# Two unread 512-column matmuls ahead of the scores of every attention unit

## The chip, the cores and the metric

The kernel runs on one core of a Trainium2 chip, as one program written by hand in Bass: each engine has its own list of instructions, and semaphores order them against each other. The metric is the device time of one execution in microseconds, of which the median of several is given. Lower is better.

## What is computed

Two transformer blocks on 256 tokens of width 1024. The first mixes three things (differential attention, an RWKV-7 time mix, attention over a memory of 256 rows) and ends in a mixture of 16 experts; the second has two layers, each with feed-forward, a mixer and feed-forward. All values are float32. What matters here are the four kinds of attention, which share one pipeline in the kernel:

```python
# first block: differential attention, 4 heads, two maps each, causal
s = einsum('bhmqd,bhmkd->bhmqk', qb, kh)          # head size 64
p = softmax(where(causal, s + bias, MASK_VALUE))
attn = p[:, :, 0] - lam * p[:, :, 1]
out = einsum('bhqk,bhke->bhqe', attn, vh)
# first block: attention over the memory, 4 heads
p = softmax(einsum('bshd,bmhd->bhsm', q, mk) * 64 ** -0.5)
# second block, even layer: dilated mixture (8 heads) and top-k attention (8 heads)
# second block, odd layer: sliding window with a learned sink per head, 16 heads
```

Around them stand products of the 256 tokens with large weight matrices: the projections into and out of each mixer, the experts and the feed-forwards.

## The kernel before

**Weights.** Every weight matrix is cut into slots of 128 rows by 3072 columns. SyncE loads them in turn into `raw`; ScalarE rounds a slot to fp32r (`w_hi`, L507) and VectorE stores the rest of the rounding (`w_lo`, L825). TensorE multiplies high by high, low by high and high by low (`mm3`, L1341 to L1343), so each product of float32 is three fp32r matmuls. The tokens lie transposed in `xT_hi` and `xT_lo`, fp32r too: 8 blocks of 128 partitions by 256 tokens each, rewritten by `norm` ahead of each group of projections.

**Attention.** The attention work is cut into 44 units. A unit is 128 query rows (tile `t`, 0 or 1) of one pair of heads, or of the two maps of one differential head; with `nk` key blocks of 128, which is `t + 1` in causal units, so that units alternate between one block (even numbers) and two (odd). The memory units always have two. Four calls of `attention(u0, u1)` run them: units 0 to 11 (8 differential, 4 memory; called the first attention below), 12 to 19 and 20 to 27 (the even layer: dilated, then top-k; the second and third), and 28 to 43 (the odd layer; the fourth). A unit goes through these steps, each on one engine:

- TensorE, `scores_unit`: two matmuls, one for each head (or map), L1403. Their operands are 64 partitions high and plain float32, and each shows in the trace as two records of 128 or 256 columns. They write PSUM banks `2 * (u % 2)` and the one after it.
- VectorE, `max_unit`: adds the bias into SBUF (L861, L864 or L870), takes the row maximum (L872), and for the fourth attention adds the sink (L875).
- ScalarE, `exp_unit`: exponential and row sum (L557), for the fourth attention that of the sink too (L560). In differential units VectorE then combines the two maps (L882 to L885).
- TensorE, `trans_unit`: transposes of 128 by 128 through the identity matrix (`flip`, L1347), into bank `4 + u % 2`.
- ScalarE, `evac_unit`: copies them to SBUF (L569).
- TensorE, `pv_unit`: probabilities by values, L1431, two records to a matmul.
- VectorE, `out_unit`: divides by the row sum and stores the result (L897 to L899, or L893).

**The order of the work** is written out by hand. TensorE's `attention` goes, for each `i`, through the scores of unit `i`, the transposes of unit `i - 2` and the product with the values of unit `i - 3`. ScalarE goes through the exponential of `i` and the evacuation of `i - 2`; VectorE through the maximum of `i`, in the second attention also two rounds of the search for the top 64 keys, and the output of `i - 4`. Each engine runs its list strictly in this order. The scores of unit `u` wait (`att_max`) until VectorE has read those of unit `u - 2`, since the two share their banks.

After an attention, `norm` transposes its result, 16 transposes at L1347, and the output projection follows.

Of the kernel before, what the change touches and what calls it, by code (L numbers as in the profile page):

```python
# [23 lines left out]
P = 128  # L24
# [72 lines left out]
def block_program(nc, wstream, x_in, mem_in, pos_in, pos_cols_in, pcol_in, prow_in, smallw_in, const_in, table_in, bias_lookup_in,  # L97
                  bias_dram, out):
    ctx = ExitStack()
    with ctx:  # L100
        def sb(name, shape, dt=F32):
            return ctx.enter_context(nc.sbuf_tensor(name, shape, dt))
# [3 lines left out]
        def S_(name):  # L106
            if name not in sems:
                sems[name] = ctx.enter_context(nc.semaphore(name))
            return sems[name]
# [5 lines left out]
        xT_hi = sb("xT_hi", [P, KD, S], F32R)  # L115
# [13 lines left out]
        ps = ctx.enter_context(nc.psum_tensor("ps", [P, 8, 512], F32))  # L129
# [1206 lines left out]
        def _(pe):  # L1336
            mm = nc.tensor.matmul
# [8 lines left out]
            def flip(out_, in_):  # L1346
                return nc.tensor.transpose(out_, in_, ident)  # L1347

            def norm(c, wait=None):
                n = norms[c]  # L1350
                if n["norm"]:
                    pe.wait_ge(S_("xs_ready"), normed[c] + 1)
                    pe.wait_ge(S_("xs1_ready"), normed[c] + 1)
                if wait:
                    pe.wait_ge(S_(wait[0]), wait[1])
                src = scaled if n["norm"] else n["src"]
                for q in range(4):
                    for k in (2 * q, 2 * q + 1):
                        for t in range(T):
                            o = S * (k % 2) + P * t  # L1360
                            ins = flip(ps[:, 4 + q, o:o + P], src[:, t, P * k:P * k + P])
                    ins.then_inc(S_("tr_ready"), 1)
# [33 lines left out]
            def scores_unit(u):  # L1396
                un = units[u]
                w, t = un["nk"] * P, un["t"]
                if u >= 2:
                    pe.wait_ge(S_("att_max"), u - 1)  # L1400
                for m in range(2):
                    o = slice(HD * m, HD * m + HD)
                    ins = mm(ps[:, 2 * (u % 2) + m, 0:w], un["q"][o, P * t:P * t + P], un["k"][o, 0:w], start=True,  # L1403
                             stop=True)
                ins.then_inc(S_("att_scores"), 1)
# [28 lines left out]
            def attention(u0, u1):  # L1434
                for i in range(u0, u1 + 3):
                    if i < u1:
                        scores_unit(i)
                    if u0 <= i - 2 < u1:
                        trans_unit(i - 2)
                    if u0 <= i - 3 < u1:  # L1440
                        pv_unit(i - 3)
# [127 lines left out]

            pe.wait_ge(S_("ident_loaded"), 16)  # L1570
            norm(0)

            pe.wait_ge(S_("const_loaded"), 16)
# [53 lines left out]
            for i in range(len(LEVELS) - 1):  # L1627

                pe.wait_ge(S_("lev_ready"), i + 1)
                for g in range(T):  # L1630
                    pe.wait_ge(S_("inv_ready"), 2 * i + g + 1)
                    for u in range(4):
                        ins = mm(ps[:, g, P * u:P * u + P], levt[i % 2][:, 4 * g + u, :], inv[:, 4 * g + u, :],  # L1633
                                 start=True, stop=True)
# [47 lines left out]
            for n in range(QKV0, MEM0):  # L1682
                proj(n)
            norm(1, ("evacuated", evac_until(MEM0 - 1)))
            for n in range(MEM0, OUT0):
                proj(n, 1 if n == MEM0 else None)
# [15 lines left out]
            pe.wait_ge(S_("qk_ready"), 2)  # L1702
            attention(*ATT1)
            norm(2, ("mixed_ready", 1))
            for n in range(OUT0, MOE0):
                proj(n, 2 if n == OUT0 else None)
# [5 lines left out]
            for k in range(KD):  # L1712
                for x in (xT_hi, xT_lo):
                    ins = mm(ps[0:20, 3, 0:S], rw[:, k, :], x[:, k, :].bitcast(F32), start=k == 0 and x is xT_hi,
                             stop=k == KD - 1 and x is xT_lo)
# [15 lines left out]
            with pe.Else():  # L1731
                pe.wait_ge(S_("gates"), 1)
                for b in range(8):
                    if b >= 2:
                        pe.wait_ge(S_("gate_ready"), b - 1)
                    for e in (2 * b, 2 * b + 1):
                        for t in range(T):
                            o = S * (e % 2) + P * t
                            ins = mm(ps[:, b % 2, o:o + P], rt_gate[:, t, e:e + 1].broadcast_to([P, P]), ident,
                                     start=True, stop=True)  # L1740
# [16 lines left out]
            for j in range(6):  # L1757
                for k in range(2):
                    ins = mm(ps[:, 5 + j // 2, S * (j % 2):S * (j % 2) + S], wq[:, k, P * j:P * j + P], cqT[:, k, :],
                             start=k == 0, stop=k == 1)  # L1760
# [180 lines left out]
```

## Time and profile before

| | |
|---|---|
| median of 3 runs | 1791.43 us (1790.6 to 1792.54) |
| the profiled execution | 1789.88 us, its span 1788.1 us |
| TensorE busy in the span | 1596.8 us, 89% |
| VectorE, ScalarE busy | 1038.3 us, 58%; 813.0 us, 45% |
| share of TensorE in the chain that ended last | 83% |
| share of the clock granted over the span | 0.911 |

Rows 1 below are of three stretches: the first attention, the second with the third, and the fourth. The profile is of one execution; the 1.8 us between its time and its span lie before the first and after the last recorded instruction. A matmul's record covers its whole way through the array, so records of matmuls that follow each other overlap: what one costs in a row of many is the distance between two starts. The granted clock is given as a share of full speed: 1.00 is 2.4 GHz and 0.50 is 1.2 GHz.

### The profile page before, as it was taken

The numbers are of one execution on the slowest core, as the hardware profiler recorded it, in microseconds if no ns is written. First come the engines' busy times: TensorE is split into PE (matmuls) and PEld (weight loads), VectorE is DVE, ScalarE is ACT, GpSimd is POOL, SyncE is SP. The second block draws the span as 40 slices with busy tenths as digits, with TensorE's granted clock in tenths as the row PEclk, the third lists the DMA queues.
The fourth block names the chain that finished last, engine by engine and source line by source line (L and its number), as shares of the span: only waits on it lengthen the run. The fifth ranks groups of instructions, "written<-read, shape, count | busy, mean of one in ns | idle before, by whom it ended". The sixth has DMA issues, their size and how long they took to land.

```text
span 1788.1 us, 29298 instructions
## 1 busy us (share of the span) xinstructions
PE 1596.8 (89%) x10458; PEld 1460.1 (82%) x10458; DVE 1038.3 (58%) x1617; ACT 813.0 (45%) x1334; POOL 41.6 (2%) x50
## 2 busy tenths in 40 slices
PE   6477868599999998999896889999899989989997
PEld 6376847488889877999895689999899988789997
DVE  3543466488879874555533745555555554555554
ACT  4311534277767763333443444433443344453342
POOL 1030000000000000000000100000000000000000
PEclk9686968799999999999998579999999998599999
DMA  6951422089979985555352055555455544055552
GB/s 225 166 52 59 141 71 71 36 284 346 350 257 350 346 324 177 176 184 195 133 181 83 1 177 176 176 181 191 150 183 177 190 135 133 2 176 179 191 194 71
DMA packets 83670, 308.02 MB, mean 172 GB/s; under 512 B 9230, under 2 KB 9358, under 8 KB 83344
## 3 DMA queue, kind: packets, MB, share of 16 engines
q1 hardware_dynamic: 79616, 289.97, 46.8%
q0 software_dynamic: 3552, 15.84, 4.8%
q10 hardware_dynamic: 432, 1.26, 0.2%
q8 instruction: 47, 0.77, 0.2%
q14 instruction: 23, 0.19, 0.0%
HBM read 299.69 MB, written 7.34 MB: 172 GB/s over the span
## 4 chain that ended last, share of the span: by engine, by line
PE 83%; DVE 9%; ACT 5%; issue 2%; DMA 1%; POOL 0%; DVEq 0%; POOLq 0%; SPq 0%; ACTq 0%
PE ps L1341 23%; PE ps L1342 23%; PE ps L1343 23%; PE ps L1347 4%; PE ps L1431 2%; DVE w_lo L825 1%; PE ps L1403 1%; ACT arena L539 1%; PE ps L1491 1%; PE ps L1566 1%; ACT w_hi L507 1%; DVE stat L872 1%; PE ps L1642 1%; ACT arena L543 1%; PE ps L1633 1%
## 5 line engine op out<-in xcount | busy, mean ns | idle before, releaser
L825 DVE TENSOR_TENSOR w_lo<-raw,w_hi 128x1024 fp32r<-128x1024 f32 x549 | 646.1, 1221 | 301.8 <-ACT w_hi L507 300.1
L507 ACT ACTIVATE w_hi<-raw 128x1024 fp32r<-128x1024 f32 x549 | 548.8, 1055 | 226.4 <-PE ps L1343 190.4
L1341 PE MATMUL ps<-xT_hi,w_hi 128*128 128x256 f32 x1656 | 470.9, 284 | 1.9 <-DVE w_lo L825 1.9
L1342 PE MATMUL ps<-xT_lo,w_hi 128*128 128x256 f32 x1656 | 469.9, 284 | 0.0
L1343 PE MATMUL ps<-xT_hi,w_lo 128*128 128x256 f32 x1656 | 469.8, 284 | 0.0
L1341 PEld LDWEIGHTS ps<-xT_hi,w_hi 128*128 128x128 f32 x1656 | 319.3, 193 | 6.8 <-issue 3.6
L1342 PEld LDWEIGHTS ps<-xT_lo,w_hi 128*128 128x128 f32 x1656 | 319.2, 193 | 3.1
L1343 PEld LDWEIGHTS ps<-xT_hi,w_lo 128*128 128x128 f32 x1656 | 318.9, 193 | 0.0
L1341 PE MATMUL ps<-w_hi,xT_hi 128*128 128x256 f32 (+2 forms) x848 | 262.0, 309 | 12.3 <-issue 8.4
L1342 PE MATMUL ps<-w_lo,xT_hi 128*128 128x256 f32 (+2 forms) x848 | 252.5, 298 | 0.0
L1343 PE MATMUL ps<-w_hi,xT_lo 128*128 128x256 f32 (+2 forms) x848 | 252.4, 298 | 0.0
L1341 PE MATMUL ps<-w_hi,h_hi 128*128 128x512 f32 x480 | 189.6, 395 | 4.3 <-DVE h_lo L982 4.3
L1347 PE MATMUL ps<-const,arena 128*128 128x128 f32 x424 | 104.5, 390 | 96.5 <-ACT arena L543 55.6
L1342 PE MATMUL ps<-w_lo,h_hi 128*128 128x512 f32 x480 | 189.4, 395 | 0.0
L1343 PE MATMUL ps<-w_hi,h_lo 128*128 128x512 f32 x480 | 187.7, 391 | 0.0
L1341 PEld LDWEIGHTS ps<-w_hi,xT_hi 128*128 128x128 f32 x848 | 162.2, 191 | 28.6 <-issue 25.9
L1347 PEld LDWEIGHTS ps<-const,arena 128*128 128x128 f32 x424 | 76.3, 205 | 117.7 <-DVE arena L845 46.3
L1342 PEld LDWEIGHTS ps<-w_lo,xT_hi 128*128 128x128 f32 x848 | 162.5, 192 | 0.1
L1343 PEld LDWEIGHTS ps<-w_hi,xT_lo 128*128 128x128 f32 x848 | 162.2, 191 | 0.0
L588 ACT ACTIVATE arena<-ps 128x256 f32<-128x256 f32 x88 | 33.9, 385 | 251.4 <-PE ps L1343 251.4
L946 DVE TENSOR_TENSOR h_hi<-ps,arena 128x256 fp32r<-128x256 f32 x88 | 37.4, 425 | 154.0 <-ACT arena L588 154.0
L1343 PEld LDWEIGHTS ps<-w_hi,h_lo 128*128 128x128 f32 x480 | 90.7, 189 | 20.1
(289 smaller groups left out, 1335.3 us busy)
## 6 DMA issues: line engine op xcount, KB each, us to landing
raw<-in_wstream SPq DMA_DIRECT2D x549, 512.0 KB, 5.0
bias_tiles<-arena POOLq DMA_DIRECT2D x2, 3072.0 KB, 52.8
arena<-bias_tiles POOLq DMA_DIRECT2D x2, 3072.0 KB, 13.3
const<-in_const ACTq DMA_DIRECT2D x1, 1112.0 KB, 10.2
smallw<-in_smallw POOLq DMA_DIRECT2D x1, 1104.0 KB, 5.5
x_res<-in_x SPq DMA_DIRECT2D x1, 1024.0 KB, 5.1
arena<-in_mem POOLq DMA_DIRECT2D x1, 1024.0 KB, 5.3
out<-arena SPq DMA_DIRECT2D x2, 512.0 KB, 2.7
```

What stands on the lines that cost most here:

```text
L507: nc.scalar.activation(w_hi[:, slot, lo:hi], raw[:, slot, lo:hi], ACT.Copy).then_inc(S_(f"hi_{part_}"), 1)
L539: ins = nc.scalar.activation(scaled[:, t, :], n["src"][:, t, :], ACT.Square, scale=D ** -0.5, accum_out=ssq[:, t:t + 1])
L543: nc.scalar.activation(scaled[:, 1, :], n["src"][:, 1, :], ACT.Copy, scale=rstd[:, 1:2]).then_inc(S_("xs1_ready"), 1)
L588: nc.scalar.activation(silu[:, f % 2, :], ps[:, 4 + f % 2, 0:S], ACT.Silu).then_inc(S_("silu_ready"), 1)
L825: tt(w_lo[:, slot, lo:hi], raw[:, slot, lo:hi], w_hi[:, slot, lo:hi].bitcast(F32), ALU.subtract).then_inc(S_(f"lo_{part_}"), 1)
L872: ins = nc.vector.tensor_reduce(nmax[:, r], dst, AX.X, ALU.max, negate=True)
L946: tt(h_hi[:, b, :], up, silu[:, b, :], ALU.mult)
L1341: a = mm(out_, stat_[0], mov[0], start=start, stop=False)
L1342: b = mm(out_, stat_[0], mov[1], start=False, stop=False)
L1343: c = mm(out_, stat_[1], mov[0], start=False, stop=stop)
L1347: return nc.tensor.transpose(out_, in_, ident)
L1431: ins = mm(o, pt[:, u % 2, m * nk + kb, :], v, start=kb == 0, stop=kb == nk - 1)
```

## The change

Ahead of the two score matmuls of each unit, and behind the wait that frees their banks, TensorE runs two fp32r matmuls of 512 columns. Both multiply the same 128 by 128 block of `xT_hi` by the first 512 columns of `xT_hi`, and write the whole of the first of the unit's two score banks. The scores then overwrite the columns they use; nothing reads the others. No wait, no semaphore and no instruction of another engine changes.

```diff
+            steady = xT_hi.rearrange("p k s -> p (k s)")
+
+            def keep_busy(out_, n):
+
+                for _ in range(n):
+                    mm(out_, xT_hi[:, 0, 0:P], steady[:, 0:out_.shape[1]], start=True, stop=True)
+
...
                 if u >= 2:
                     pe.wait_ge(S_("att_max"), u - 1)
+                keep_busy(ps[:, 2 * (u % 2), :], 2)
                 for m in range(2):
```

TensorE's list in the fourth attention, before: scores of a unit with two key blocks (L1403, 128x256), four transposes of another (L1347), values of a third (L1431, 128x64), scores of a unit with one key block, and so on.

```order
4555 L1403 MATMUL ps<-arena 128x256 x2
4556 L1347 MATMUL ps<-const,arena 128x128 x4
4557 L1431 MATMUL ps<-arena 128x64 x2
4558 L1403 MATMUL ps<-arena 128x128 x2
4559 L1347 MATMUL ps<-const,arena 128x128 x2
4560 L1431 MATMUL ps<-arena 128x64 x4
4561 L1403 MATMUL ps<-arena 128x256 x2
```

The same place now, where the lines of the program have moved on by seven or eight (L1411 are the scores, L1439 the values, L1354 the added matmuls).

```order
4574 L1354 MATMUL ps<-xT_hi 128x512 x2
4575 L1411 MATMUL ps<-arena 128x256 x2
4576 L1347 MATMUL ps<-const,arena 128x128 x4
4577 L1439 MATMUL ps<-arena 128x64 x2
4578 L1354 MATMUL ps<-xT_hi 128x512 x2
4579 L1411 MATMUL ps<-arena 128x128 x2
4580 L1347 MATMUL ps<-const,arena 128x128 x2
4581 L1439 MATMUL ps<-arena 128x64 x4
4582 L1354 MATMUL ps<-xT_hi 128x512 x2
4583 L1411 MATMUL ps<-arena 128x256 x2
```

Nothing has moved against anything else; 44 pairs of matmuls have come in, 88 in all, one pair ahead of each unit's scores.

## Rows read from the trace of the kernel before

**Rows 1.** Windows: busy us of PE, PEld, DVE, ACT, POOL; clock; DMA share, GB/s.

```profile
252.70:286.00 33.30, 26.29 (x132) 17.89 (x132) 25.41 (x73) 18.56 (x62) 0.00 (x0) 0.69 0.00 0
979.00:1040.40 61.40, 49.30 (x208) 37.50 (x208) 41.26 (x125) 23.18 (x82) 7.89 (x8) 0.50 0.00 1
1504.30:1556.30 52.00, 47.35 (x208) 35.61 (x208) 28.93 (x96) 24.49 (x97) 0.00 (x0) 0.55 0.02 6
```

**Rows 2.** Chain that ended last, fourth attention: start us, us, what.

```profile
1533.86 1.18 PE ps L1403 x4
...
1538.42 1.97 PE ps L1431 x8
```

**Rows 3.** Timeline of TensorE, two units: start us, us, what, [idle before].

```profile
1540.32 1.23 PE L1403 MATMUL ps<-arena 64*128 64x256 f32 x4
1541.47 1.11 PE L1347 MATMUL ps<-const,arena 128*128 128x128 f32 x4
1542.38 0.95 PE L1431 MATMUL ps<-arena 128*128 128x64 f32 x4
1543.26 0.80 PE L1403 MATMUL ps<-arena 64*128 64x128 f32 x4
1543.99 0.69 PE L1347 MATMUL ps<-const,arena 128*128 128x128 f32 x2
1544.95 1.97 PE L1431 MATMUL ps<-arena 128*128 128x64 f32 x8 [0.27 <-ACT arena L569]
1546.85 1.23 PE L1403 MATMUL ps<-arena 64*128 64x256 f32 x4
```

**Rows 4.** Timeline of TensorE where the clock is at 1.00.

```profile
277.75 0.70 PE L1403 MATMUL ps<-arena 64*128 64x256 f32 x4
278.39 0.66 PE L1347 MATMUL ps<-const,arena 128*128 128x128 f32 x4
...
1551.48 1.10 PE L1431 MATMUL ps<-arena 128*128 128x64 f32 x8 [1.19 <-ACT arena L569]
1552.43 0.61 PE L1347 MATMUL ps<-const,arena 128*128 128x128 f32 x4
```

**Rows 5.** Timeline of TensorE, fp32r matmuls at clock 0.50, then at 1.00.

```profile
169.93 0.52 PE L1341 MATMUL ps<-w_hi,xT_hi 128*128 128x384 f32 x1
170.25 0.52 PE L1342 MATMUL ps<-w_lo,xT_hi 128*128 128x384 f32 x1
...
1420.55 0.40 PE L1341 MATMUL ps<-w_hi,h_hi 128*128 128x512 f32 x1
1420.79 0.40 PE L1342 MATMUL ps<-w_lo,h_hi 128*128 128x512 f32 x1
```

**Rows 6.** Windows of 1 us around two changes of the clock.

```profile
1505.00:1506.00 1.00, 0.22 (x4) 0.00 (x0) 0.93 (x4) 0.55 (x1) 0.00 (x0) 1.00 0.02 4
1506.00:1507.00 1.00, 0.75 (x4) 0.45 (x4) 0.97 (x2) 0.97 (x5) 0.00 (x0) 0.56 0.00 0
1550.00:1551.00 1.00, 0.29 (x2) 0.00 (x0) 0.82 (x5) 1.00 (x6) 0.00 (x0) 0.75 0.00 0
```

**Rows 7.** Timeline of TensorE: pairs of units in the first and the third attention.

```profile
262.31 1.23 PE L1403 MATMUL ps<-arena 64*128 64x256 f32 x4
...
267.59 1.23 PE L1403 MATMUL ps<-arena 64*128 64x256 f32 x4
...
1023.75 1.23 PE L1403 MATMUL ps<-arena 64*128 64x256 f32 x4
...
1030.00 1.23 PE L1403 MATMUL ps<-arena 64*128 64x256 f32 x4
```

**Rows 8.** Window of 20 us in the second attention.

```profile
980.00:1000.00 20.00, 13.06 (x54) 8.49 (x51) 18.65 (x58) 7.54 (x29) 0.00 (x0) 0.50 0.01 1
```

**Rows 9.** TensorE timeline and window: 16 transposes of `norm`, later in the program.

```profile
1465.82 3.28 PE L1347 MATMUL ps<-const,arena 128*128 128x128 f32 x16 [5.63 <-ACT arena L543]
...
1468.00:1469.00 1.00, 1.00 (x8) 1.00 (x7) 1.00 (x3) 0.98 (x3) 0.00 (x0) 0.71 0.00 0
```

## The prediction

> **What bounds the kernel now.** I read the windows over the attention stages first, because the change touches nothing else. They last 33.3, 61.4 and 52.0 us, 147 us of 1788, and their granted clock is 0.69, 0.50 and 0.55 [rows 1], where the whole span has 0.911: TensorE runs most of its attention work at 1.2 GHz, although in the fourth it is busy for 47.35 of 52.00 us. Next the chain of waits there [rows 2], which goes round once in two units. The scores of a unit with two key blocks (1.18 us) are followed by VectorE's bias and maximum and ScalarE's exponential and evacuation, and then by eight records of the product with the values (1.97 us), behind which the next such scores stand at once. From the end of the scores to the start of the values lie 1538.42 - (1533.86 + 1.18) = 3.38 us, in which the chain is on VectorE and ScalarE, whose work no TensorE clock changes.
>
> The timeline of TensorE shows the same round from inside [rows 3]: 6.53 us from scores to scores (1540.32 to 1546.85), made of scores 1.15, four transposes 0.91, values 0.88, short scores 0.73, two transposes with a wait 0.96, long values 1.90. TensorE is thus nearly full at the half clock, with some 0.5 us of slack in the 0.96 (two transposes take half of the 0.91 that four take). Engine and chain are almost equally long, so either a faster clock or more work on TensorE is felt.
>
> **What the change costs at each clock.** It removes nothing and moves nothing. It adds 88 matmuls. At full clock 512 columns of fp32r take 1420.79 - 1420.55 = 0.24 us [rows 5], taken as 0.23 since starts are rounded and others of this run stand 0.23 apart, so a pair takes 0.46 us. At half clock 384 columns take 0.32 us [rows 5], so 512 take 0.43 and a pair 0.85 us. Both pairs of a round stand in TensorE's list. The one ahead of the long scores lies on the chain, the other beside VectorE's and ScalarE's 3.38 us, as far as there is slack. Queued behind the added matmuls are the scores, for which VectorE waits, and on the other engines nothing else.
>
> *Clock stays at 0.50.* TensorE's own work in a round is 6.53 - 0.5 = 6.03 us, with 4 x 0.43 = 1.7 added 7.73: TensorE alone sets the round, and it grows by 1.2 us. The fourth attention has some seven such rounds: +8.4 us. The third has a round of 6.25 us [rows 7], so with the same TensorE work +1.5, in four rounds +6.0.
>
> *Clock goes to 1.00.* The long scores then take 278.39 - 277.75 = 0.64 us, the long values 1552.43 - 1551.48 = 0.95 [rows 4]; transposes and short work halve as well and vanish beside the chain. The gap before the long values, which is 3.47 us from the first transpose (1544.95 - 1541.47), stays: in the one place where it was run at full clock TensorE waited 1.19 us there on the evacuation [rows 4]. A round is 3.47 + 0.95 + 0.46 + 0.64 = 5.5 us, 1.03 less than now: 7 rounds, -7.2 us. The second added pair lies in the gap (0.44 + 0.46 values + 0.46 added + 0.4 scores + 0.2 transposes = 2.0 of 3.47) and costs nothing; were that cover gone it would cost 0.46. In the third attention the round is 0.28 us shorter to begin with, so 5.5 - 0.28 = 5.2 instead of 6.25, four times: about -4.0.
>
> *First attention.* A differential pair takes 267.59 - 262.31 = 5.28 us [rows 7], and of it 25.41 of 33.30 us is VectorE's [rows 1], so less is to be had. At full clock the round would lose half of scores and values (about 1.0 us) and gain 0.46: -0.57, in the three rounds that are at the half clock now -1.7; but in its two memory rounds, which already run at 1.00 in part (rows 4, first row), the pair on the chain costs 0.46 each. Together -0.8. Entirely at half clock it would be about +0.85 in four rounds, +1.2 in two, and 2 us for the full clock lost there: +7.8. *Second attention.* VectorE is busy for 18.65 of 20 us [rows 8], with the search for the top keys. TensorE's 13.06 us have room for two to three pairs; its round of about 7.2 us comes close to 7.7 at half clock, so 0 to +1.6; I take +0.8. *Behind the last unit* of each attention come values and transposes with no added matmuls; two long values, one short and four transposes are 1.9 + 1.9 + 0.9 + 0.9 = 5.6 us at half clock, so up to 3 us are saved in one of them if the full clock lasts that long, and nothing if not. I take -1.
>
> **Which clock it will be.** Here the trace gives hints and no price. The fourth attention starts at 1.00 and loses it around 1506, when TensorE has just stood idle between its first scores: it is busy for 0.22 us from 1505 to 1506, still at 1.00, and has 0.56 in the next microsecond [rows 6]. Within 1550 to 1551 the clock comes back by itself, after transposes and short values that followed each other closely. In the first attention it comes and goes twice. So the mix of the attention is close to what holds the clock, on the low side of it. The projections, fp32r in full columns without a pause, always have 1.00 after their start. The change adds such work: at full clock 0.92 us of it in 5.5 us, 17%; at half clock 1.7 in 7.7, 22%. Its first two pairs fall right where the clock is lost today. That speaks for a held clock. Against it: at full clock the round has a gap of 3.47 - 2.0 = 1.5 us each time, longer than the idle time in the microsecond ahead of the loss at 1506. I therefore take the clock as held for three quarters of the third and fourth attention.
>
> The Trainium skill ("TensorE: Matmul & The Clock Gate", Part 4: PE-mode transpose) says that a transpose does not count as busy in the way a matmul does and that the full clock does not engage for it. By that the six transposes in a round would help nothing and the added pairs would have to hold the clock nearly alone, which speaks against this change. The trace disagrees: the clock rises from 0.50 within 1468 to 1469, when for 2.7 us nothing but the 16 transposes of `norm` had run [rows 9].
>
> **The sum.** Fourth attention 0.75 x 7.2 - 0.25 x 8.4 = -3.3; third 0.75 x 4.0 - 0.25 x 6.0 = -1.5; first -0.8; second +0.8; behind the last units -1.0. Together -5.8 us. The profiled execution took 1789.88 us and would take 1784.1. It lies 1.55 us under the median, so against the median of 1791.43 the forecast is 1785.6 us.
>
> **The rivals.**
> - *Held throughout.* -7.2 - 4.0 - 0.8 + 0 - 3.0 = -15.0: 1776.4 us. For it: all 16 units of the fourth attention begin under full clock. Against: the 1.5 us gaps.
> - *Held half the time.* Fourth +0.6, third +1.0, first about +1.5, second +0.8, tails 0: +3.9, 1795.3 us; with a little more of it, no change. The break-even lies at a share of 8.4 / (8.4 + 7.2) = 54% in the fourth attention.
> - *Never held, the slower side.* The added pairs are too thin for the clock and TensorE is the bound in every round: +8.4 + 6.0 + 7.8 + 1.6 = +23.8, 1815.2 us. The place is the long round of the fourth attention, the price 1.2 us in it; it decides once the clock is at 0.50 for over 46% of it. For it: TensorE was already busy for nine tenths of the stage and still at half clock. Against: the two rises without any help. Were the skill's sentence on transposes to hold here, this is the case that would come out.
> - *It does not do what it says.* The added pairs leave the clock as it is, but hide in part, because the scores' weight loads and their wait overlap them: half of the +23.8, some 1803 us.
>
> **How the numbers follow.** Forecast 0.40, held throughout 0.24, half the time 0.15, never 0.13, hidden in part 0.08. A measurement of this kernel can tell about 0.2%, 3.6 us, from no change, so faster means under 1787.8. Faster: all of the second, nine tenths of the first, a little of the third, 0.61. Same: the edge of the first and half of the third, 0.15. Slower 0.24. The range leaves out the case that is never held, the far end of the one that hides in part and the very best of the second: 1773 to 1806.
>
> **What would show it.** In the windows of the changed kernel the granted clock of the fourth attention should be around 0.85 and no longer 0.55, that of the third around 0.8, and the distance from long scores to long scores should be 5.5 us under full clock and 7.7 under half. The wait of the long values on the evacuation (L569) should grow from 0.27 to 1.5 us. If rounds at full clock stay at 6.5 us, the chain was read wrongly; if the clock is at 0.50, only the slower side is left.

## The result and the profile after

The changed kernel takes 1796.29 us (median of 13 runs, 1790.00 to 1803.29), the kernel before in the same session 1791.46 us (13 runs, 1789.66 to 1793.59). The ratio is 1.0028, 95% interval [1.0018, 1.0038]: slower by 4.8 us, small but measurable. The time lies inside the range that was given, on the side that was given 24%. The forecast was faster by 5.8 us. One execution of a later run (e15, 1879.63 us at a granted clock of 0.795 over the span) was in a slower state that no other execution here shows; it is left out of that run's median and ratio.

The page of the changed kernel, its line of busy time and its clock over 40 slices:

```profile
PE 1601.8 (89%) x10546; PEld 1454.7 (81%) x10546; DVE 1038.6 (58%) x1617; ACT 812.8 (45%) x1334; POOL 41.7 (2%) x50
PEclk9686979799999999999998589999999999899999
```

The profiled execution took 1795.32 us, 5.4 more than that of before, with a granted clock of 0.926 over the span, where before had 0.911. So TensorE had more of its full clock and the kernel was slower. The windows of the changed kernel, over the first, second, third and fourth attention, each from its first added pair to the `norm` (or the next attention's pair) behind it, columns as in [rows 1]:

```profile
253.43:292.57 39.14, 29.56 (x157) 18.79 (x157) 28.99 (x77) 18.74 (x63) 0.00 (x0) 0.83 0.00 0
...
984.17:1020.02 35.85, 30.76 (x120) 20.68 (x121) 28.89 (x91) 12.24 (x41) 1.95 (x2) 0.60 0.00 0
1020.02:1047.87 27.85, 24.27 (x122) 16.53 (x122) 12.54 (x34) 10.89 (x40) 6.01 (x6) 0.75 0.01 1
1512.64:1562.06 49.42, 41.04 (x240) 28.02 (x240) 28.63 (x96) 24.14 (x97) 0.00 (x0) 0.90 0.01 3
```

Measured in the same way, those of before last 37.09, 35.12, 26.22 and 52.03 us. The clock rose in all four stages (before: 0.69, 0.50, 0.50, 0.55), yet only the fourth is shorter, by 2.6 us; the first is 2.05 longer, the second 0.73, the third 1.63. Together that is +1.8 us. These are two executions, and a stage without added work is not the same in each: over the profiles of all runs that add nothing there, the first attention took 36.7 to 38.8 us, the second and third together 60.6 to 61.5, and the fourth 52.0 to 53.5. In the change and in its repetition (e12) they took 39.1, 63.5 to 63.7, and 49.4 to 49.6 us. So the sign of each stage stands, but the first attention's 2.05 could as well be 0.4.

Each attention can be cut in three on TensorE's timeline: its **head**, from the first scores or added pair to the scores of its unit 3; its **rounds**, from there to the scores of its last unit; and its **tail**. In us:

| | first | second | third | fourth | sum |
|---|---|---|---|---|---|
| before: head, rounds, tail | 4.2, 20.9, 12.1 | 8.2, 15.7, 11.2 | 3.3, 12.5, 10.4 | 3.4, 39.2, 9.5 | 150.5 |
| the change | 6.7, 20.4, 12.1 | 9.4, 16.1, 10.4 | 7.5, 11.3, 9.0 | 4.8, 35.0, 9.6 | 152.3 |

The heads grew by 2.6 + 1.2 + 4.2 + 1.5 = 9.4 us (the terms are rounded), rounds and tails shrank by 7.6. This is the head of the third attention, first before:

```profile
1014.19 2.58 PE L1403 MATMUL ps<-arena 64*128 64x128 f32 x12
1016.89 0.69 PE L1347 MATMUL ps<-const,arena 128*128 128x128 f32 x2
1017.50 1.23 PE L1403 MATMUL ps<-arena 64*128 64x256 f32 x4
```

and then in the changed kernel (scores at L1411, added pairs at L1354):

```profile
1020.02 1.20 PE L1354 MATMUL ps<-xT_hi 128*128 128x512 f32 x2
1021.15 0.80 PE L1411 MATMUL ps<-arena 64*128 64x128 f32 x4
1021.88 1.22 PE L1354 MATMUL ps<-xT_hi 128*128 128x512 f32 x2
1023.03 1.23 PE L1411 MATMUL ps<-arena 64*128 64x256 f32 x4
1024.19 1.22 PE L1354 MATMUL ps<-xT_hi 128*128 128x512 f32 x2
1025.34 0.80 PE L1411 MATMUL ps<-arena 64*128 64x128 f32 x4
1026.07 0.69 PE L1347 MATMUL ps<-const,arena 128*128 128x128 f32 x2
1026.41 1.20 PE L1354 MATMUL ps<-xT_hi 128*128 128x512 f32 x2
1027.55 1.23 PE L1411 MATMUL ps<-arena 64*128 64x256 f32 x4
```

Four pairs follow each other with nothing but scores and two transposes between, at half clock, 1.13 to 1.15 us from a pair's start to the scores behind it. Nothing of this attention is running yet that they could hide beside: its whole pipeline waits for these scores.

A round of the fourth attention, where the clock is at 1.00, is what the forecast described:

```profile
1541.02 0.70 PE L1411 MATMUL ps<-arena 64*128 64x256 f32 x4
1541.66 0.66 PE L1347 MATMUL ps<-const,arena 128*128 128x128 f32 x4
1542.15 0.56 PE L1439 MATMUL ps<-arena 128*128 128x64 f32 x4
1542.52 0.71 PE L1354 MATMUL ps<-xT_hi 128*128 128x512 f32 x2
1543.16 0.49 PE L1411 MATMUL ps<-arena 64*128 64x128 f32 x4
1543.58 0.44 PE L1347 MATMUL ps<-const,arena 128*128 128x128 f32 x2
1545.13 1.10 PE L1439 MATMUL ps<-arena 128*128 128x64 f32 x8 [1.11 <-ACT arena L569]
1546.05 0.71 PE L1354 MATMUL ps<-xT_hi 128*128 128x512 f32 x2
```

From the first transpose to the long values lie 1545.13 - 1541.66 = 3.47 us, against 1544.95 - 1541.47 = 3.48 in [rows 3], now with 1.11 us of waiting in it. The scores behind the last row start at 1546.69, so the round is 5.67 us, against 6.53 before. The chain that ended last goes through the added pair:

```profile
1539.46 1.10 PE ps L1439 x8
1540.57 0.52 PE ps L1354 x2
1541.09 0.66 PE ps L1411 x4
```

### The profile page after: what moved, and what is told of

Same layout as the page of the kernel before. It is cut to its first block, busy times and chain, and to the rows that moved or that the text cites. A ratio compares the mean times of both kernels' runs of the same rounds, so it can differ in the third digit from the quotient of the medians.

```text
span 1793.5 us, 29474 instructions
## 1 busy us (share of the span) xinstructions
PE 1601.8 (89%) x10546; PEld 1454.7 (81%) x10546; DVE 1038.6 (58%) x1617; ACT 812.8 (45%) x1334; POOL 41.7 (2%) x50
## 4 chain that ended last, share of the span: by engine, by line
PE 83%; DVE 8%; ACT 5%; issue 2%; DMA 1%; POOL 0%; DVEq 0%; POOLq 0%; SPq 0%; ACTq 0%
PE ps L1341 23%; PE ps L1342 23%; PE ps L1343 23%; PE ps L1347 3%; PE ps L1439 2%; DVE w_lo L825 1%; PE ps L1411 1%; ACT arena L539 1%; PE ps L1354 1%; PE ps L1499 1%; ACT w_hi L507 1%; PE ps L1574 1%; DVE stat L872 1%; PE ps L1650 1%; ACT arena L543 1%
## 5 line engine op out<-in xcount | busy, mean ns | idle before, releaser
L1341 PE MATMUL ps<-w_hi,xT_hi 128*128 128x256 f32 (+2 forms) x848 | 261.7, 309 | 12.4 <-issue 8.4
L1347 PE MATMUL ps<-const,arena 128*128 128x128 f32 x424 | 97.3, 369 | 93.9 <-ACT arena L543 55.6
L1347 PEld LDWEIGHTS ps<-const,arena 128*128 128x128 f32 x424 | 72.3, 194 | 110.5 <-DVE arena L845 46.3
L946 DVE TENSOR_TENSOR h_hi<-ps,arena 128x256 fp32r<-128x256 f32 x88 | 37.4, 425 | 154.3 <-ACT arena L588 154.3
## 6 DMA issues: line engine op xcount, KB each, us to landing
bias_tiles<-arena POOLq DMA_DIRECT2D x2, 3072.0 KB, 52.7
```

The lines of the kernel that those rows point to most:

```text
L946: tt(h_hi[:, b, :], up, silu[:, b, :], ALU.mult)
L1341: a = mm(out_, stat_[0], mov[0], start=start, stop=False)
```

## The experiments

All edits are to the changed kernel, most of them a condition on the added line. Each session had its own runs of the kernel before.

**One attention at a time.**

```diff
-                keep_busy(ps[:, 2 * (u % 2), :], 2)
+                if u >= ATT4[0]:                  # e1; e2: u < ATT1[1]; e3: ATT1[1] <= u < ATT4[0]
+                    keep_busy(ps[:, 2 * (u % 2), :], 2)
```

> The pair of added matmuls stands only ahead of the units of the fourth attention (28 to 43). Theory P (the change pays where it holds the clock and where TensorE was the bound, and loses elsewhere): the profile after has this stage 2.6 us shorter (52.0 to 49.4 us) with the clock at 0.93 in it, so 1791.5 - 2.6 = 1788.9 us, with a spread of some 3 us between executions. Rival Q (the loss of the change is a fixed cost of every added pair, spread evenly over 44 units): 16 of 44 units of +4.8 us, so 1793.2 us.

> The pair stands only ahead of units 0 to 11. Theory P: this stage was bound by VectorE and by the chain; the profile after has it 2.0 us longer, so +1.5 to +2.5, 1793.5 us. Rival Q: 12 of 44 of +4.8, +1.3, 1792.8 us. Rival R (the loss lies in other stages, as routing, where the clock falls differently because everything has moved): +0, 1791.5 us.

> The pair stands only ahead of units 12 to 27, the second and third attention, which are entered at half clock. Theory P: 61.3 us became 63.7 us in the profile after, and other executions are worse when the clock comes later: +2.4 to +7, 1796 us, and the spread between executions, 13 us for the whole change, is mostly here. Rival Q: 16 of 44, +1.7, 1793.2 us.

Against 1791.86 us: e1 1789.05 us (ratio [0.9966, 0.9988]), e2 1793.81 ([0.9995, 1.0016]), e3 1795.49 ([1.0005, 1.0024]). By the medians the pairs in the fourth attention gain 2.8 us, those in the second and third cost 3.6, and those in the first some 2 that the interval doesn't separate from nothing. Theory P foretold e1 and e3; the even spread of rival Q is out for e1, and e2 can't tell the theories apart. The stages have the same signs, in the order e1 (fourth attention), e2 (first), e3 (second with third, then the fourth):

```profile
1504.62:1554.60 49.98, 41.45 (x240) 28.31 (x240) 28.61 (x96) 24.15 (x97) 0.00 (x0) 0.89 0.01 5
```

```profile
252.87:292.29 39.42, 29.85 (x156) 18.64 (x156) 28.95 (x77) 18.76 (x63) 0.00 (x0) 0.86 0.00 0
```

```profile
982.24:1045.99 63.75, 55.07 (x240) 37.25 (x241) 41.42 (x125) 23.15 (x81) 7.97 (x8) 0.66 0.00 1
1510.70:1564.15 53.45, 48.90 (x209) 37.19 (x209) 28.90 (x96) 24.50 (x97) 0.00 (x0) 0.52 0.01 4
```

In e3 the stages with pairs are 2.4 us longer than in the profile of before. The fourth attention has none there and is 1.4 us longer too, so the 3.6 us are not all the price of the pairs where they stand.

**Two attentions at a time, and the change once more.** The conditions are `u < ATT4[0]` (e13), `u >= ATT1[1]` (e14), `u < ATT1[1] or u >= ATT4[0]` (e15), and none (e12).

> The change as it is, all 44 units, beside its three halves on the same chip. The ratios of the parts (fourth alone -4.1 us, first alone +1.1, middle alone +2.7) add up to about 0, while the whole was at +5.0 us. Theory S (the parts add, and the first measurement of the whole or those of the parts were unlucky): 1790 to 1793 us beside 1791.5. Rival I (the parts do not add, since each one moves where the clock stands at the entry of the next): again 1795 to 1798 us.

> The pairs in units 0 to 27, not in the fourth attention. Theory S: +1.1 + 2.7 = +3.8, 1795.3 us. Rival I: the whole less the fourth's gain, +5.0 + 4.1 = +9, 1800 us.

> The pairs in units 12 to 43, not in the first attention. Theory S: +2.7 - 4.1 = -1.4, 1790.1 us. Rival I: +4, 1795.5 us, if it is the middle that spoils the fourth.

> The pairs in units 0 to 11 and 28 to 43, not in the second and third attention. Theory S: +1.1 - 4.1 = -3.0, 1788.5 us. Rival I: between -3 and +2 us, if it is the first that spoils the fourth.

Against 1791.55 us: e12 1796.38 ([1.0017, 1.0043]), so the result repeats; e13 1799.73 ([1.0029, 1.0055]); e14 1796.69 ([1.0009, 1.0033]); e15 1792.46 ([0.9993, 1.0011]). Rival I came out in all four, theory S in none: the parts do not add. By medians the three come to -2.8 + 2.0 + 3.6 = +2.8 singly and +4.8 together; the first and the middle to +5.6 and +8.2; the middle and the fourth to +0.8 and +5.1. Each median can be off by some 2 us, so it is the ratios that carry this, and only two of the comparisons are clear: they give -4.1, +1.1 and +2.7 us singly, -0.3 in all against +5.4 in e12, and -1.4 against +3.8 for the middle and the fourth (e14). One way in which this comes about shows in the fourth attention of e14's profile, which has the same instructions as in e1 (scores at L1412, values at L1440):

```profile
1508.88:1564.88 56.00, 50.19 (x241) 35.40 (x241) 28.82 (x96) 24.34 (x97) 0.00 (x0) 0.72 0.01 3
1523.00:1528.00 5.00, 4.53 (x30) 3.13 (x30) 2.88 (x12) 2.15 (x10) 0.00 (x0) 1.00 0.00 0
1533.00:1538.00 5.00, 5.00 (x24) 4.12 (x22) 3.29 (x12) 2.39 (x10) 0.00 (x0) 0.50 0.00 0
```

It takes 56.0 us at 0.72, where the change, e1, e12 and e15 took 49.4 to 50.1 at 0.89 to 0.91. Its full-clock rounds are 5.66 us, as in the change. Then the clock falls and stays down, and TensorE, busy for all of the third window's 5 us, has rounds of 1539.23 - 1531.41 = 7.82 us:

```profile
1531.41 1.23 PE L1412 MATMUL ps<-arena 64*128 64x256 f32 x4
...
1534.19 1.20 PE L1354 MATMUL ps<-xT_hi 128*128 128x512 f32 x2
...
1536.54 1.81 PE L1440 MATMUL ps<-arena 128*128 128x64 f32 x8
1538.10 1.20 PE L1354 MATMUL ps<-xT_hi 128*128 128x512 f32 x2
1539.23 1.23 PE L1412 MATMUL ps<-arena 64*128 64x256 f32 x4
```

Whether the clock is held with this filling thus differs from one execution to another, and a stage that loses it is 6 us longer. The 13 executions of the change spread over 13 us, those of before over 4. With e12 the change has 22 executions, in two groups: 15 took 1790.0 to 1796.9 us with a granted clock over the span of 0.925 to 0.930, and 7 took 1800.5 to 1803.3 with 0.921 or 0.922. A fourth attention as in e14's profile would lower the clock over the span by an estimated (56.0 x 0.28 - 49.4 x 0.10) / 1795 = 0.006, which fits the step between the groups; no execution of the second group was traced, so this is argued. Either way the first group alone has a median of 1795.3 us, some 4 us above before: the slow group puts only 1 us on the median of the change.

**How much is added, in the fourth attention alone.** One matmul instead of two (e11), four (e8), two of 128 columns (e7), and the pair ahead of the short units only, where it is off the chain (e4).

```diff
+                if u >= ATT4[0]:                  # e4: and u % 2 == 0
+                    keep_busy(ps[:, 2 * (u % 2), :], 2)   # e11: 1, e8: 4; e7: 0:P in place of the last :
```

> The pair stands only ahead of the units with one key block of the fourth attention (28, 30, ... 42), where TensorE has a gap behind it at full clock; the pair on the chain, ahead of the long scores, is gone. If the clock is held as well by half as many matmuls, a round at full clock is 5.67 - 0.64 = 5.0 us and the stage about 45 us, 1784 to 1786 us. If eight pairs are too few for the clock, the rounds at half clock grow by 1.15 - 0.5 = 0.65 us and the time is 1791 to 1796 us.

> As the run on the fourth attention alone, but the two matmuls have 128 columns and not 512. It measures what two matmuls cost apart from their columns: if columns were all, 2 x 0.11 = 0.2 us at half clock; if there is a fixed cost of some 0.3 us in going over from fp32r at 128 rows to float32 at 64 rows, 0.5 us from the start of the pair to the start of the scores. The clock should not be held: 0.5 to 0.6 in the stage, and the time 1793 to 1797 us.

> As the run on the fourth attention alone, but four matmuls of 512 columns. If the added work decides whether the clock is held, it is held throughout (0.95 or more), with a small spread between executions, but a round is 0.46 us longer than with two at full clock: stage 51 to 53 us, 1791 to 1793 us. If the clock falls all the same, when the chain leaves TensorE idle, the share stays at 0.89.

> One matmul of 512 columns, not two, ahead of the scores of the fourth attention alone. At full clock it costs about 0.64 - 0.23 = 0.41 us, so a round held would be 5.4 us. If the share of added work decides, the clock is held for less of the stage than with two (0.89) and four (0.98): 0.6 to 0.75, and as half-clock rounds grow to 7.0 us the time is 1791 to 1795 us. If one is enough, 0.9 and 1787 us.

| added ahead of each unit of the fourth attention | clock there | stage, us | median, before in its session, us |
|---|---|---|---|
| nothing | 0.55 | 52.0 | |
| two of 128 columns (e7) | 0.58 | 55.7 | 1795.33, 1791.95 |
| one of 512 (e11) | 0.58 | 56.5 | 1796.76, 1791.19 |
| two of 512, short units only (e4) | 0.75 | 49.5 | 1791.68, 1791.86 |
| two of 512 (e1) | 0.89 | 50.0 | 1789.05, 1791.86 |
| four of 512 (e8) | 0.98 | 51.8 | 1792.33, 1791.95 |

```profile
1505.99:1562.51 56.52, 53.19 (x225) 38.77 (x225) 28.92 (x96) 24.51 (x97) 0.00 (x0) 0.58 0.01 4
```

```profile
1506.98:1558.77 51.79, 44.79 (x273) 31.78 (x273) 29.02 (x96) 24.50 (x97) 0.00 (x0) 0.98 0.01 4
```

The rows are those of e11 and e8. The first row is of one execution, and other profiles with nothing added there gave 52.7 to 53.5 us at 0.52 to 0.55. With one matmul or with two short ones the price is paid and next to no clock comes back, less than the 0.6 to 0.75 that was expected of e11; with four the clock is held and its gain eaten up again. Of the amounts tried ahead of every unit two is the best, and it is thin. In the profile of e4 the clock was at 1.00 for its first rounds of 5.15 us and then fell for the rest of the stage; that profiled execution was the fastest of its 11 runs (1786.66 us), and its median is no different from before.

**The same kind of work in another place.** In the changed kernel TensorE waits 1.1 us in every full-clock round for the evacuation (L569) ahead of the long values. Here the fp32r work, three matmuls of 384 columns, stands ahead of that wait, and no pair ahead of the scores. It writes the columns of the values' bank that the values don't use.

```diff
-                keep_busy(ps[:, 2 * (u % 2), :], 2)
...
-                pe.wait_ge(S_("att_pt"), u + 1)
...
+                if u >= ATT4[0]:                  # e6: ATT1[1] <= u < ATT4[0]; e9: u >= ATT1[1]; e10: all
+                    keep_busy(ps[:, 6 + u % 2, P:512], 3)
+                pe.wait_ge(S_("att_pt"), u + 1)
```

> No pair ahead of the scores. In the fourth attention alone, each unit has three matmuls of 384 columns ahead of the wait for its evacuated transposes (in columns 128 to 511 of the bank that the product with the values is about to use), where TensorE stands idle for over 1 us in a round at full clock. Theory G (the added work is free in the gap, and its nearly even spread holds the clock): a round at full clock is 5.67 - 0.64 = 5.0 us, the stage 44 to 46 us, the time 1784 to 1786 us. Rival H (the clock is lost as in the run with half the pairs; three matmuls cost 1.2 us in a round at half clock): the stage is 50 to 55 us, the time 1790 to 1795 us.

> The same three matmuls of 384 columns ahead of the wait for the transposes, in units 12 to 27 alone, which are entered at half clock. Theory G: the second attention is bound by VectorE and has idle time for them; the clock comes up in it or early in the third, whose 26 us become some 23; the time is 1789 to 1791 us, and better than the 1795.5 us with the pairs ahead of the scores. Rival H: at half clock 1.2 us per unit do not fit beside VectorE and the clock comes late, 1794 to 1797 us.

> The three matmuls of 384 columns in the gap, in units 12 to 43. If the two gains add (-9.4 for the fourth attention, -3.0 for the second and third): 1779.5 us, with a spread no wider than in those runs. If the gain of the one depends on when the other ends: anything from 1778 to 1786 us.

> The same in all 44 units. In the first attention VectorE and the chain set the pace and a round at full clock is about 0.6 us shorter than at half clock; added work that is free in the gap would give -1 to -2 us on top of the run without it: 1778 us. If the first attention has no such gap (its product with the values follows the transposes of differential units closely), 0 to +1 us, 1780 us.

Against 1791.95 us: e5 1782.53 ([0.9948, 0.9975]), e6 1788.97 ([0.9978, 0.9996]). Against 1791.19 us: e9 1782.74 ([0.9934, 0.9961]), e10 1780.93 (1778.91 to 1782.09, ratio [0.9927, 0.9954]). The last beats both kernels: 10.3 us under before, 15 under the change. Theory G held in e5 and e6, and e5 came out even shorter than it said. The fourth attention of e5 and its TensorE (scores at L1410, values at L1440):

```profile
1506.81:1549.83 43.02, 37.81 (x257) 29.11 (x257) 28.36 (x96) 24.04 (x97) 0.00 (x0) 1.00 0.02 7
```

```profile
1530.76 0.70 PE L1410 MATMUL ps<-arena 64*128 64x256 f32 x4
...
1533.77 0.80 PE L1354 MATMUL ps<-xT_hi 128*128 128x384 f32 x3
1534.88 1.11 PE L1440 MATMUL ps<-arena 128*128 128x64 f32 x8 [0.31 <-ACT arena L569]
1535.91 0.70 PE L1410 MATMUL ps<-arena 64*128 64x256 f32 x4
```

The added three end inside the wait, which shrinks from 1.11 to 0.31 us. The round is 5.15 us, 0.52 less than in the change, and its chain, of which this is a part, has no row of L1354 any more between 1525 and 1537 us:

```profile
1529.73 1.10 PE ps L1440 x8
1530.84 0.66 PE ps L1410 x4
...
1531.51 0.70 DVE arena L870
```

The place and the amount differ at once here, 3 x 384 = 1152 columns against 2 x 512 = 1024. The fourth attention is 7.0 us shorter than in e1; its six rounds at 0.52 and its head, 3.3 us instead of 4.8, are the place and make 4.7 of it. Whether the rest, a clock of 1.00 instead of 0.89, comes from the place or from the columns was not separated.

The four attentions of e10 take 140.2 us together, 10.25 less than before. The profiled executions differ by 8.5 and the medians by 10.3, so the attentions account for the gain and 1.7 us in other stages go against it in the profiles. These gains do not add either: e5 and e6 come to -12.4, e9, which is both, to -8.5; its fourth attention had a clock of 0.92, that of e5 1.00.

**The heads.** To test whether the four first units of each attention are where the change loses, the pairs were left out there (e16), or kept there alone (e17).

```diff
+                if u - max(s for s in (0, 12, 20, 28) if s <= u) >= 4:    # e17: < 4
+                    keep_busy(ps[:, 2 * (u % 2), :], 2)
```

> The pairs stay, but not in the first four units of each of the four attentions. Theory of the heads: in the traces of the kernel before and of the change the distance from the first scores (or added pair) of an attention to the scores of its unit 3 grew by 2.6, 1.2, 4.2 and 1.5 us, 9.4 together, because those pairs stand in a row with scores for which all other engines wait. Without them the first attention falls back to about its 37 us, the third loses about 4 and the fourth 1.5, and the time is 1796.3 - 9.4 = 1787 us, if the clock later on is as in the change. Rival, the heads set the clock: the fourth attention loses the clock in its head as in the kernel before, stays at 1.2 GHz with the pairs and has rounds of 7.8 us, its stage takes 56 us or more, and the time is 1796 us or above.

> The pairs stand in the first four units of each attention alone. Theory of the heads: they are a cost without a return, up to 9.4 us in all, less what the clock gives back: 1797 to 1801 us, the same growth of the four heads as in the change (2.6, 1.2, 4.2 and 1.5 us). Rival, the heads set the clock: the fourth attention keeps the full clock past its head, runs rounds of 5.2 instead of 6.5 us and takes 46 us or less, and the time is at most 1792 us.

Against 1791.39 us: e16 1797.26 ([1.0021, 1.0043]), e17 1798.07 ([1.0025, 1.0043]). In e17 the heads last 6.8, 9.4, 7.5 and 4.8 us, longer by 2.6, 1.2, 4.2 and 1.5 as in the change, so the price is shown: 9.4 us. In e16 they last 4.2, 8.2, 3.3 and 3.3 again, but the time did not come down by 9.4: its rounds and tails are 3.5 us longer than those of before, where the change's are 7.6 shorter. Of these 11.0 us the third attention has 4.5 and the fourth 4.7. The third shows why. Windows of e16 over its rounds, then of e17 over its head and its rounds:

```profile
1017.27:1033.01 15.74, 15.74 (x61) 11.24 (x61) 6.09 (x16) 7.40 (x29) 5.13 (x5) 0.50 0.01 1
```

```profile
1018.63:1026.12 7.49, 7.49 (x24) 3.81 (x23) 3.52 (x8) 2.39 (x11) 2.37 (x3) 0.51 0.00 0
1026.12:1035.84 9.72, 7.03 (x53) 5.38 (x52) 5.44 (x14) 5.96 (x24) 3.59 (x4) 1.00 0.01 2
```

Entered at half clock without pairs in the head, the rounds of e16 stay there, filled to the brim, 15.7 us instead of 12.5. With the head alone the clock comes back at its end and the rounds take 9.7. The head thus buys the clock and costs more than that clock returns: 4.2 us against 2.8 + 0.4 in e17. Neither theory of this pair of runs was right in full. The one of the heads had e17 right and missed e16 by 10 us. The rival had the time of e16, though its fourth attention took 52.5 us and not the 56 it named, and missed e17. The price of the heads is 9.4 us, and leaving them out does not save it.

## Why the prediction was wrong, by its own steps

**The reading of what bounds the kernel held.** The round at full clock was forecast as 5.5 us and is 5.67; at half clock as 7.7 and is 7.82; the wait on L569 was to grow to 1.5 us and grew to 1.12; the gap of 3.48 us (the prediction has 3.47) stayed. The price of a pair in a round was forecast as 0.46 us at full clock and is 5.67 - 5.15 = 0.52 (change against e5), and e8, whose round is 1537.69 - 1531.56 = 6.13 us, puts the next pair at 0.46. Nor were transposes in the way of the clock: it was at 1.00 over all of the fourth attention of e5, with six of them in every round.

**The failed step: the sum had no term for the heads.** It counted a round for every two units, "some seven" in the fourth and four in the third attention, and priced each pair as a pair in a round, where something covers half of them. But the first four units of an attention are no round: from the scores of unit 3 to those of the last unit the fourth has six rounds and the third two, and what the sum took for further rounds is head and tail. No values stand beside the first pairs. In the third attention all four are on the path, and there each costs more than 0.85 us at half clock: 1.13 to 1.15. In the second, where TensorE waits for VectorE in the head, most of their time is covered (+1.2 us); in the first and the fourth (+2.6 and +1.5) part of it is made up for by a clock that is higher in the head than before. In the rounds part of a pair's 1.13 us is made up for, since the long values followed by scores took 1.90 us [rows 3], and followed by a pair take 1538.10 - 1536.54 = 1.56; in the head no long values stand before a pair. The Trainium skill ("TensorE: Matmul & The Clock Gate", Part 1, "Wait — 56ns, not 53.3ns?") gives 426.7 ns for 512 columns back to back at the slow clock, so 0.85 us for a pair; by it the four would cost an estimated 3.4 us, and the third attention measured 4.2. The trace agrees for the second matmul of a pair (1.13 us in place for two, 0.70 for one in e11); what a pair takes beyond its columns this figure does not cover.

Term by term, in us, forecast against the change's profile:

| | forecast | measured |
|---|---|---|
| fourth attention | -3.3 | rounds -4.2, head +1.5 |
| third | -1.5 | rounds -1.2, head +4.2 |
| first | -0.8 | rounds -0.5, head +2.6 |
| second | +0.8 | rounds +0.5, head +1.2 |
| tails | -1.0 | -2.1 |
| sum | -5.8 | rounds and tails -7.6, heads +9.4: +1.8 |

Rounds and tails alone came within 2 us of the forecast. That they did was partly luck: "held for three quarters" was too low for the fourth attention (0.90), and there were six rounds to gain from and not seven, two and not four in the third.

**The clock.** For the third attention 0.8 was forecast and 0.75 came, but not as thought: it is entered at half clock, and its head has to be run through before the clock rises. The prediction gave the mechanism "held half the time" 15% and +3.9 us; the time is right, the reason another. What it lacked was that the clock comes out differently in each execution (0.921 to 0.930 over the span), so that a share of three quarters is a mean over executions that differ by 13 us. The Trainium skill (same page, Part 1, "What's actually happening") says that how many matmuls run slow varies from run to run of one kernel and calls the penalty of one ramp less than 1% of a typical span. The spread here is 13 us, 0.7% of the time: within that sentence, and nearly three times what was to be measured.

**What stays open.** The profiles differ by 5.4 us, the attentions by 1.8. The other 3.6 lie in stretches that no edit touches: 2.3 us in the experts' routing, 0.7 ahead of the first attention, 0.9 between the third and the fourth, -0.3 behind the fourth. Such stretches vary by themselves. The one of the routing took 35.1 us in the profile of before, 37.4 in that of the change, and up to 37.5 in e3 and e14, whose added work all comes later. The clock falls and rises at other places in it. So 1.8 us of the 4.8 are placed, and for the other 3 no trace here shows a cause. A clock lost in the fourth attention can't be the main part of them, since the faster of the two groups above is itself some 4 us slower than before. Whether pairs in the first attention make the longer routing more frequent was not found either. What decides in an execution whether the clock is held, and how an earlier attention acts on it, stays open.

## What to carry over

Work that is to hold the clock belongs where the engine waits for others, ahead of the wait and not ahead of the instruction that others wait for: here the same kind of work, three matmuls of 384 columns for two of 512, gave -10.3 us in the one place and +4.8 in the other. Before counting rounds, look at the first units of a pipeline apart, since little there covers an addition. And where a gain hangs on the clock, look at the spread of the executions and at several profiles: a stage of the same instructions took 49.4 or 56.0 us.

## What the runs showed of the hardware

- TensorE can be busy for 53.19 of 56.52 us and be granted 0.58 (e11), for 15.74 of 15.74 us and be granted 0.50 (e16), and for 37.81 of 43.02 us and be granted 1.00 (e5). The share of busy time alone does not tell the clock.
- With nothing, one, two and four matmuls of 512 columns ahead of each unit of the fourth attention, one profile each, the granted clock was 0.55, 0.58, 0.89 and 0.98. It is not the amount alone: two ahead of every other unit gave 0.75 (e4), and the same two ahead of every unit gave 0.72 in the profile of e14.
- A pair of 512 columns ahead of scores takes 1.13 us to their start at half clock, 0.27 more than 2 x 0.43; one such matmul takes 0.70 (e11), again 0.27 more. Two of 128 columns take 0.60 (e7), an estimated 0.39 more than their columns. So the extra time is there in each case and is not the same for each shape.
- In the third attention of e16, at half clock, TensorE was busy all the time; in that of the change, with the same list in the rounds and the clock at 1.00, it waited 0.25 and 0.83 us for the evacuation in its two rounds.
